# Convolution sums in PSUM, window biases built beside their GEMM, and a late norm in token halves, in a chain of transformer blocks on one Trainium2 core

## The chip, the cores and the metric

The program runs on 1 core of one Trainium2 chip (trn2). The metric is the device time in microseconds (us) of one execution, lower is better; the figure of a kernel is the median of its runs.

## What is computed

The reference runs two blocks on one sequence of 512 tokens of 1024 features, all in f32. The first has two layers: a bidirectional gated delta net (GDN) and a dilated window attention, each followed by a squared-ReLU MLP. The second has two layers with a context of 256 tokens: a Fourier and Hyena mixer and a latent attention (MLA), each followed by a gated feed forward part with a short convolution. Cut to what the change touches:

```python
# first block, layer 0: the input projection of the GDN (24 tiles of q, k, v and 8 of the gate z)
qkv = silu(short_conv(h @ w_in[:, :QKV], conv_w))      # 5 taps, per feature
# first block, layer 1: windows of 128, 512, 2048 tokens, dilated by 1, 4, 16
scores = q @ k.T * scale + rel_bias[bucket(distance)]  # 6 heads per window
# second block, last layer: only the 512 tokens of x are left
h = rms_norm(x, norm2) * (1 + scale) + shift
gate, val = split(h @ w_up)                            # 2 x 2816 features
x = x + g2 * ((silu(dwconv3(gate) + b) * val) @ w_down)
```

## The kernel before, in words

**Layout and stages.** Activations stay in SBUF with features on the 128 partitions and tokens along a row. The program is a list of stages. Each stage (`Core.stage`, L149) is one block with a program for each engine, which talk by semaphores, and it ends with a barrier of all engines; nothing of the next stage starts before it.

**GEMMs.** A weight matrix is cut into chunks of 128x1024 f32 (512 KB). SP loads them in order into a ring of 4 slots (`stream_weights`, `_load`, L188); it runs up to 4 chunks ahead of the stage, into the next GEMM too. For precision each chunk is split into a high and a low fp32r part: ACT copies the high part (`split_high`, L201) and POOL subtracts it for the low part (`split_low`, L207), each into 2 slots, so the high part of chunk n waits until the chunk n-2 has been multiplied. PE multiplies three products per 128x128 block: low weights by high activations (L258), high by low (L259), high by high (L260) (`product`). One output tile of 128 features is one chunk: 8 blocks, so 24 matmuls of 512 columns, each with its own weight load. `multiply_tiles` (L262 to L288) runs the tiles over a ring of 4 PSUM banks (0 to 3); a tile waits until VectorE (DVE) has drained the tile 4 before it (`drained`). With two streams of activations, the matmuls of stream 1 follow those of stream 0 in each tile, and stream 1 has 2 banks (4 and 5).

**Norms.** `Norm` (L306 on) makes the RMS norm first: squares, a sum over the partitions by a matmul with ones (L336), a root on ACT (L340), a reciprocal on DVE, the scaled values (L396), then the shift and the high part on ACT (L365, L366) and the low part on DVE (L390). `LateNorm` (L406 on) multiplies by the gain alone: high part on ACT (L428), low part on DVE (L457); the squares and the root run beside the first two tiles, and 1/rms is applied when a tile is drained (`drain`, L469 and L472), together with two more columns of the GEMM that carry the shift.

**The stage gdn_in** (`gdn_in_stage`, L629 on): DVE copies a tile with its 1/rms into a padded row in SBUF (L665), then sums the 5 taps: a tensor_scalar (L671) and four scalar_tensor_tensor (L673), each in the tile `conv_sum` in SBUF and each waiting for the one before it (class `Order`). ACT takes the Silu of the sum (L703). DVE may start tile n when the Silu of tile n-2 is done. ACT's program is in order: the high part of chunk n+4, then the wait for the sums of tile n and its Silu. After the 24 convolved tiles DVE writes the normed activations for a later stage (`normed`, L480), then drains the 8 gate tiles (L685).

**The stage window_bias** (`window_bias_stage`, L1616 to L1673) stands alone ahead of the GEMM of the windows. SP loads four small tables; PE spreads the bias table by distance (3 matmuls, L1653); DVE adds the window mask (L1674); SP stores the rows to DRAM and reads them back so that each partition is shifted by one element (L1640 to L1645, DRAM to SBUF); PE turns the order of the partitions with a flip matrix (10 matmuls of 384 columns, L1660) and ACT copies them out (L1666). The stage window_in (`copy_gemm_stage`, L1678 on) then multiplies 27 tiles with a `LateNorm`.

**The feed forward part of the last layer** (`ffn_stages`, L2371 on): 22 pairs of tiles, a gate and a value. In layer 0 there are two streams (512 tokens of x, 256 of the context) and a `LateNorm`; in layer 1 (stages ffn1_up and ffn1_down) one stream of 512 tokens, a `Norm` and 2 banks. Two streams of this kind multiply 512 columns and 258 columns (256 tokens and the 2 columns of the shift).

Of the kernel before, what the change touches and what calls it, by code (L numbers as in the profile page):

```python
# [13 lines left out]
P = 128  # L14
T = 512
# [94 lines left out]
class Core:  # L110
# [151 lines left out]
    def multiply_tiles(self, pe, g, streams, drained, norm):  # L262
# [366 lines left out]
def gdn_in_stage(core, g, norm, parts, conv, gate_z, loads):  # L629
# [3 lines left out]
    with ExitStack() as ctx:  # L633
        padded = core.sb("conv_padded", [P, 2, T + 2 * PAD], ctx)
        acc = core.sb("conv_sum", [P, 2, T], ctx)
        taps = core.params("conv").rearrange("p (n j) -> p n j", j=CONV)
        TAPS_ORDER = CONV * g.per
        with core.stage("gdn_in", "loaded", "drained", "convolved", "silued", "dve_order", *Norm.SIGNALS) as (
# [14 lines left out]
            def _(dve):  # L653
# [28 lines left out]
                for n in range(QKV_TILES, g.tiles):  # L682
                    core.tile_sums(dve, g, n)
                    dve.wait_ge(silued, n + 1)
                    dve.tensor_tensor(acc[:, n % 2, :], core.ps[n % RING][:, :], core.rstd[:, 0, :], ALU.mult).then_inc(convolved, 1)  # L685
# [8 lines left out]
            def _(act):  # L694
# [4 lines left out]
                def tile(n, at, turn, out):  # L699
# [3 lines left out]
                    act.activation(out, acc[:, at % 2, :], ACT.Silu).then_inc(silued, 1)  # L703
# [912 lines left out]
def window_bias_stage(core, a, bias0, bias12):  # L1616
# [3 lines left out]
    scratch = core.nc.dram_tensor("bias_by_distance", [HG, 8 * P], F32, kind="Internal").ap()  # L1620
    WIDTHS = (4 * P, 2 * P, 2 * P)
    with ExitStack() as ctx:
        rel = core.sb("rel_table", [BUCKETS, 3 * HG], ctx)
        hot = core.sb("rel_onehot", [BUCKETS, 8 * P], ctx)
        mask = core.sb("window_mask", [HG, 8 * P], ctx)
        rows = core.sb("bias_rows", [HG, 8 * P], ctx)
        flip = core.sb("flip", [P, P], ctx)
        rising0, rising12 = core.sb("rising0", [P, HG, 3 * P], ctx), core.sb("rising12", [P, 2, HG, P], ctx)

        flat12 = lambda t, n: t[:, n // 2, (n % 2) * (HG // 2):(n % 2 + 1) * (HG // 2), :].rearrange("p h j -> p (h j)")  # L1630
        FLIPS = [(rising0[:, h, :], bias0[:, h, :], 3 * P) for h in range(HG)]
        FLIPS += [(flat12(rising12, n), flat12(bias12, n), HG // 2 * P) for n in range(4)]
        with core.stage("window_bias", "loaded", "spread", "masked", "stored", "laid", "flipped", "kept") as (
# [15 lines left out]
            def _(pe):  # L1649
# [7 lines left out]
                for n, (src, _dst, w) in enumerate(FLIPS):  # L1657
                    if n >= 4:
                        pe.wait_ge(kept, n - 3)
# [1691 lines left out]
```

## Time and profile before

| | |
|---|---|
| runs | 3608.68, 3605.53, 3614.42 us, median 3608.68 |
| the profiled execution | 3603.65 us, of which the span is 3601.9 us |
| busy over the span | PE 3231.5 us (90%), PE weight loads 2466.0 (68%), DVE 1620.1 (45%), ACT 1020.0 (28%), POOL 1096.4 (30%) |
| granted TensorE clock | mean 0.943 of full speed |
| DMA | 282.14 MB, 78 GB/s |

A profile row of a group names line, engine and operation, what it writes and reads, how often, its busy time and the mean of one. An idle time is put down to what ended it. A row of the timeline has the start from the beginning of the span, the duration of the merged instructions, engine, line, operation, and how many there are.

### The profile page before, as it was taken

The numbers are of one execution on the slowest core, as the hardware profiler recorded it, in microseconds if no ns is written. First come the engines' busy times: TensorE is split into PE (matmuls) and PEld (weight loads), VectorE is DVE, ScalarE is ACT, GpSimd is POOL, SyncE is SP. The second block draws the span as 40 slices with busy tenths as digits, with TensorE's granted clock in tenths as the row PEclk, the third lists the DMA queues.
The fourth block names the chain that finished last, engine by engine and source line by source line (L and its number), as shares of the span: only waits on it lengthen the run. The fifth ranks groups of instructions, "written<-read, shape, count | busy, mean of one in ns | idle before, by whom it ended". The sixth has DMA issues, their size and how long they took to land. (4 is left out here: it accounts for less than half of the span.)

```text
span 3601.9 us, 53210 instructions
## 1 busy us (share of the span) xinstructions
PE 3231.5 (90%) x20636; PEld 2466.0 (68%) x20636; DVE 1620.1 (45%) x2230; ACT 1020.0 (28%) x1524; POOL 1096.4 (30%) x518
## 2 busy tenths in 40 slices
PE   7887877999979979999798889999999679979999
PEld 5664766787858757878377458888888333358877
DVE  7853543421121534211576247556555355544531
ACT  3322322222222612222120013222223224433322
POOL 3322211444424124444022012222232005534443
PEclk9987998999989979999799999999999879989999
DMA  3215434222222012222212101111111011012222
GB/s 124 76 47 177 143 114 159 88 99 87 99 78 99 30 47 88 99 88 94 91 47 77 59 26 57 64 63 61 57 62 56 33 46 44 23 64 94 98 88 87
DMA packets 78393, 282.14 MB, mean 78 GB/s; under 512 B 9305, under 2 KB 12191, under 8 KB 77228
## 3 DMA queue, kind: packets, MB, share of 16 engines
q1 hardware_dynamic: 77676, 279.52, 23.3%
q8 instruction: 103, 1.69, 0.2%
q10 hardware_dynamic: 576, 0.62, 0.1%
q14 instruction: 38, 0.31, 0.0%
HBM read 270.12 MB, written 2.12 MB: 76 GB/s over the span
## 5 line engine op out<-in xcount | busy, mean ns | idle before, releaser
L207 POOL TENSOR_TENSOR weights_low<-weight_ring,weights_high 128x1024 fp32r<-128x1024 f32 x359 | 897.4, 2500 | 1891.0 <-ACT weights_high L201 1891.0
L201 ACT ACTIVATE weights_high<-weight_ring 128x1024 fp32r<-128x1024 f32 x372 | 391.6, 1053 | 742.9 <-PE bank L260 726.7
L258 PE MATMUL bank<-ffn_in_high,weights_low 128*128 128x512 f32 (+1 forms) x1056 | 376.7, 357 | 14.0 <-DVE ffn_in_low L390 9.0
L259 PE MATMUL bank<-ffn_in_low,weights_high 128*128 128x512 f32 (+1 forms) x1056 | 376.1, 356 | 0.0
L260 PE MATMUL bank<-ffn_in_high,weights_high 128*128 128x512 f32 (+1 forms) x1056 | 376.1, 356 | 0.0
L258 PEld LDWEIGHTS bank<-ffn_in_high,weights_low 128*128 128x128 f32 x1056 | 200.1, 189 | 47.1 <-issue 12.4
L259 PEld LDWEIGHTS bank<-ffn_in_low,weights_high 128*128 128x128 f32 x1056 | 200.1, 189 | 28.2
L260 PEld LDWEIGHTS bank<-ffn_in_high,weights_high 128*128 128x128 f32 x1056 | 199.2, 189 | 28.1
L258 PE MATMUL bank<-mlp_down_high,weights_low 128*128 128x512 f32 x512 | 201.3, 393 | 8.4 <-DVE mlp_down_low L557 8.4
L258 PE MATMUL bank<-mlp_in_high,weights_low 128*128 128x512 f32 x512 | 200.9, 392 | 7.3 <-DVE mlp_in_low L457 6.2
L259 PE MATMUL bank<-mlp_down_low,weights_high 128*128 128x512 f32 x512 | 200.7, 392 | 0.0
L260 PE MATMUL bank<-mlp_down_high,weights_high 128*128 128x512 f32 x512 | 200.6, 392 | 0.0
L259 PE MATMUL bank<-mlp_in_low,weights_high 128*128 128x512 f32 x512 | 200.0, 391 | 0.0
L260 PE MATMUL bank<-mlp_in_high,weights_high 128*128 128x512 f32 x512 | 199.9, 390 | 0.0
L258 PE MATMUL bank<-ffn_down_high,weights_low 128*128 128x512 f32 (+1 forms) x528 | 189.6, 359 | 11.4 <-DVE ffn_down_low L557 11.4
L259 PE MATMUL bank<-ffn_down_low,weights_high 128*128 128x512 f32 (+1 forms) x528 | 189.5, 359 | 0.0
L260 PE MATMUL bank<-ffn_down_high,weights_high 128*128 128x512 f32 (+1 forms) x528 | 188.2, 357 | 0.0
L557 DVE TENSOR_TENSOR ffn_down_low<-ffn_hidden,ffn_down_high 128x1024 fp32r<-128x1024 f32 (+1 forms) x66 | 101.6, 1569 | 190.4 <-ACT ffn_down_high L514 190.4
L557 DVE TENSOR_TENSOR mlp_down_low<-mlp_hidden,mlp_down_high 128x512 fp32r<-128x512 f32 x64 | 44.1, 692 | 295.0 <-ACT mlp_down_high L514 295.0
L258 PE MATMUL bank<-gdn_in_high,weights_low 128*128 128x512 f32 x256 | 106.8, 417 | 43.9 <-DVE gdn_in_low L457 19.8
L619 DVE SCALAR_TENSOR_TENSOR mlp_relu<-bank,rstd 128x512 f32<-128x512 f32 x64 | 44.2, 691 | 214.0 <-PE bank L260 213.5
L673 DVE SCALAR_TENSOR_TENSOR conv_sum<-conv_padded,params,conv_sum 128x512 f32<-128x512 f32 x96 | 118.7, 1237 | 13.9 <-DVE conv_sum L671 0.2
(546 smaller groups left out, 6426.8 us busy)
## 6 DMA issues: line engine op xcount, KB each, us to landing
weight_ring<-in_mod SPq DMA_DIRECT2D x96, 512.0 KB, 4.6
weight_ring<-in_ffn_up SPq DMA_DIRECT2D x88, 512.0 KB, 3.3
weight_ring<-in_mlp_up SPq DMA_DIRECT2D x64, 512.0 KB, 3.3
weight_ring<-in_mlp_down SPq DMA_DIRECT2D x64, 512.0 KB, 3.3
weight_ring<-in_ffn_down SPq DMA_DIRECT2D x44, 512.0 KB, 3.3
weight_ring<-in_gdn_in SPq DMA_DIRECT2D x32, 512.0 KB, 3.3
weight_ring<-in_dswa_in SPq DMA_DIRECT2D x27, 512.0 KB, 3.3
weight_ring<-in_fh_in SPq DMA_DIRECT2D x16, 512.0 KB, 3.3
```

The costliest lines, as they stand in the source:

```text
L201: act.activation(self.high[:, (g.s0 + at) % SPLIT, 0:g.floats], raw, ACT.Copy).then_inc(self.high_ready, 1)
L207: pool.tensor_tensor(self.low[:, slot, 0:g.floats], self.ring[:, (g.c0 + at) % RING, 0:g.floats], self.high[:, slot, 0:g.floats], ALU.subt ...
L258: pe.matmul(bank, wl, ah, start=start, stop=False)
L259: pe.matmul(bank, wh, al, start=False, stop=False)
L260: return pe.matmul(bank, wh, ah, start=False, stop=stop)
L557: last = dve.tensor_tensor(low[:, at % 2, :, lo:lo + tokens], src((n - p * PER_PASS) * KC, KC), high[:, at % 2, :, lo:lo + tokens], ALU.su ...
L619: dve.scalar_tensor_tensor(out=relu[:, at % 2, :], in0=core.ps[at % RING][:, :], scalar=0.0, in1=core.rstd[:, 0, :], op0=ALU.max, op1=ALU. ...
L673: ins = dve.scalar_tensor_tensor(out=acc[:, b, :], in0=padded[:, b, t:t + T], scalar=tap, in1=acc[:, b, :], op0=ALU.mult, op1=ALU.add)
```

## The change

Three edits. (1) In gdn_in the tile `conv_sum` in SBUF is gone; the sums of the taps, and the gate tiles, are written to PSUM banks 4 and 5. (2) The stage window_bias is gone; its steps are a class `DistanceBias` that runs inside window_in: SP loads the tables ahead of the weights, stores the rows after chunk 16 has been asked for and reads them back four chunks later; PE does the 3 matmuls of the table after tile 3 and the 10 flips behind the last tile, with 3 banks in turn in place of 4; DVE adds the mask after draining tile 3; ACT copies the flips out after its last weight split. (3) ffn1_up takes the path that layer 0 had: a `LateNorm` over two streams, here the first and the second 256 tokens of x, with 4 and 2 banks, the drains through `drain`, and the shift added on DVE.

```diff
@@ multiply_tiles
             if n == 1 and norm.late:
                 norm.tensor(pe)
+        if beside:
+            beside.tensor(pe)
         rounds(pe, RING, g.count, RING, tile)
@@ gdn_in_stage
-        acc = core.sb("conv_sum", [P, 2, T], ctx)
+        acc = core.ps[4:6]
...
-                                order(dve.tensor_scalar(acc[:, b, :], padded[:, b, 0:T], tap, None, ALU.mult))
+                                order(dve.tensor_scalar(acc[b][:, :], padded[:, b, 0:T], tap, None, ALU.mult))
...
-                                ins = dve.scalar_tensor_tensor(out=acc[:, b, :], in0=padded[:, b, t:t + T], scalar=tap,
-                                                               in1=acc[:, b, :], op0=ALU.mult, op1=ALU.add)
+                                ins = dve.scalar_tensor_tensor(out=acc[b][:, :], in0=padded[:, b, t:t + T], scalar=tap,
+                                                               in1=acc[b][:, :], op0=ALU.mult, op1=ALU.add)
...
-                    act.activation(out, acc[:, at % 2, :], ACT.Silu).then_inc(silued, 1)
+                    act.activation(out, acc[at % 2][:, :], ACT.Silu).then_inc(silued, 1)
@@ window_bias_stage becomes class DistanceBias
+        self.to = [core.ps[b][:, 0:3 * P] for b in (4, 5, 7)]
+        self.banks = [core.ps[4][0:HG, 0:4 * P], core.ps[5][0:HG, 0:2 * P], core.ps[5][0:HG, 2 * P:4 * P]]
...
+    def turn(self, pe):
+        pe.wait_ge(self.laid, 48)
+        for n, (src, _) in enumerate(self.flips):
+            if n >= len(self.to):
+                pe.wait_ge(self.kept, n - len(self.to) + 1)
+            pe.matmul(self.to[n % len(self.to)], self.flip[:, :], src, start=True, stop=True).then_inc(self.flipped, 1)
@@ copy_gemm_stage
         def _(sp):
+            beside.load(sp)
+            core.stream_weights(sp, g.c0 + g.count // 2)
+            beside.store(sp)
+            core.stream_weights(sp, g.c0 + g.count // 2 + RING)
+            beside.lay(sp)
             core.stream_weights(sp, g.c0 + g.count)
...
             core.split_high_all(act, g, norm)
+            beside.keep(act)
...
-            core.multiply_tiles(pe, g, [(parts, core.ps[0:RING])], drained, norm)
+            core.multiply_tiles(pe, g, [(parts, core.ps[0:RING])], drained, norm, beside)
+            beside.turn(pe)
...
-            rounds(dve, 0, g.tiles, g.per, tile)
+            rounds(dve, 0, RING, g.per, tile)
+            beside.vector(dve)
+            rounds(dve, RING, g.tiles, g.per, tile)
@@ ffn_stages
-    streams = [0, 1] if with_ctx else [0]
-    xs, tokens = (core.x, core.xc if with_ctx else None), (T, TC)
+    streams = [0, 1]
+    first, of_mod = (T, streams) if with_ctx else (T // 2, [0, 0])
+    xs = (core.x[:, :, 0:first], core.xc[:, :, :] if with_ctx else core.x[:, :, first:T])
+    tokens, to = (first, TC if with_ctx else T - first), (0, first)
...
-                            o(dve.tensor_scalar(gates[0], bank(0, j, 0)[:, :], 1.0, None, ALU.mult))
-                            dve.sem_inc(gate_drained, 1)
...
-                            dve.wait_ge(silued, m + 1)
-                            dve.tensor_tensor(dsts[0], gate[0], bank(0, j, 1)[:, :], ALU.mult).then_inc(gated, 1)
-                            dve.wait_ge(gated, m + 1)
-                            dve.sem_inc(value_drained, 1)
```

## Rows read from the trace of the kernel before

**Rows 1.** Busy time in windows, gdn_in: length, PE, PEld, DVE, ACT, POOL, clock, DMA

```profile
38.00:204.00 166.00, 146.50 (x594) 111.75 (x593) 145.18 (x146) 53.41 (x59) 61.58 (x25) 0.98 0.24 78
```

**Rows 2.** Waits of that stretch (40 to 205 us): total us, times, longest

```profile
ACT conv L703 <- DVE conv_sum L673: 87.4, 18, 5.3
```

**Rows 3.** Timeline of DVE in gdn_in

```profile
38.45 0.69 DVE L665 TENSOR_TENSOR conv_padded<-bank,rstd 128x512 f32<-128x512 f32 x1 [0.23 <-DVE rstd L464]
...
87.69 0.49 DVE L671 TENSOR_SCALAR conv_sum<-conv_padded,params 128x512 f32<-128x512 f32 x1 [0.28 <-ACT conv L703]
88.32 5.32 DVE L673 SCALAR_TENSOR_TENSOR conv_sum<-conv_padded,params,conv_sum 128x512 f32<-128x512 f32 x4
94.53 0.49 DVE L671 TENSOR_SCALAR conv_sum<-conv_padded,params 128x512 f32<-128x512 f32 x1 [0.28 <-ACT conv L703]
...
203.88 7.50 DVE L480 SCALAR_TENSOR_TENSOR gdn_h<-x,params,rstd 128x512 f32<-128x512 f32 x8
```

**Rows 4.** Lines L673 and L665: durations in ns, min/median/max, first and last start

```profile
L673 DVE SCALAR_TENSOR_TENSOR conv_sum<-conv_padded,params,conv_sum x96: 750/752/2803, 40.1 to 203.2; 128x512 f32<-128x512 f32 x96
...
L665 DVE TENSOR_TENSOR conv_padded<-bank,rstd x24: 679/684/691, 38.4 to 197.1; 128x512 f32<-128x512 f32 x24
```

**Rows 5.** Timeline of PE in gdn_in, the last gate tiles

```profile
212.19 0.77 PE L258 MATMUL bank<-gdn_in_high,weights_low 128*128 128x512 f32 x1 [4.64 <-DVEq L687]
...
220.03 0.39 PE L258 MATMUL bank<-gdn_in_high,weights_low 128*128 128x512 f32 x1
...
227.03 0.39 PE L258 MATMUL bank<-gdn_in_high,weights_low 128*128 128x512 f32 x1
...
235.89 0.40 PE L260 MATMUL bank<-gdn_in_high,weights_high 128*128 128x512 f32 x1
```

**Rows 6.** Groups of DVE, busy us, mean ns, and one of PE weight loads

```profile
L575 DVE SCALAR_TENSOR_TENSOR x<-bank,mod,x 128x512 f32<-128x512 f32 x32 | 22.9, 747 | 24.5 <-PE bank L260 24.5
...
L2446 DVE TENSOR_SCALAR ffn_padded<-bank 128x512 f32<-128x512 f32 x22 | 15.3, 693 | 84.9 <-PE bank L260 84.9
...
L258 PEld LDWEIGHTS bank<-ffn_in_high,weights_low 128*128 128x128 f32 x1056 | 200.1, 189 | 47.1 <-issue 12.4
```

**Rows 7.** Timeline of window_bias and of the ends of window_in: SP, PE, ACT, DVE

```profile
1017.49 0.34 SPq L1638 DMA_DIRECT2D rel_table<-in_rel_table  x1
...
1020.77 3.45 PE L1653 MATMUL bank<-rel_onehot,rel_table 32*6 32x512 f32 x6 [4.70 <-DMA flip<-in_flip]
...
1037.75 8.52 PE L1660 MATMUL bank<-rising,flip 128*128 128x384 f32 x20 [13.53 <-DMA rising<-bias_by_distance]
...
1042.44 0.49 ACT L1666 ACTIVATE bias<-bank 128x384 f32<-128x384 f32 x1 [0.15 <-PE bank L1660]
...
1046.31 0.49 ACT L1666 ACTIVATE bias<-bank 128x384 f32<-128x384 f32 x1 [0.15 <-PE bank L1660]
1047.52 5.01 ACT L428 ACTIVATE window_in_high<-x,params 128x512 fp32r<-128x512 f32 x8 [0.72 <-PEq L157]
...
1202.04 0.69 DVE L1706 TENSOR_TENSOR window_qkv<-bank,rstd 128x512 f32<-128x512 f32 x1 [4.80 <-PE bank L260]
```

**Rows 8.** Timeline of ffn1_up: ACT at its start, PE in tile 0 and at the end

```profile
3204.78 1.06 ACT L201 ACTIVATE weights_high<-weight_ring 128x1024 fp32r<-128x1024 f32 x1 [5.84 <-PEq L157]
...
3232.53 0.50 PE L258 MATMUL bank<-ffn_in_high,weights_low 128*128 128x512 f32 x1 [0.31 <-DVE ffn_in_low L390]
...
3467.03 0.39 PE L260 MATMUL bank<-ffn_in_high,weights_high 128*128 128x512 f32 x1
```

**Rows 9.** Timeline of ffn0_up: ACT at its start, PE at 258 and 512 columns

```profile
2198.08 5.01 ACT L428 ACTIVATE ffn_in_high<-x,mod_gain 128x512 fp32r<-128x512 f32 x8 [9.19 <-PEq L157]
...
2227.59 0.39 PE L258 MATMUL bank<-ffn_in_high,weights_low 128*128 128x258 f32 x1 [1.46 <-DVEq L2441]
...
2236.09 0.28 PE L258 MATMUL bank<-ffn_in_high,weights_low 128*128 128x258 f32 x1
...
2238.99 0.39 PE L258 MATMUL bank<-ffn_in_high,weights_low 128*128 128x512 f32 x1
```

More of the change, by code:

```diff
@@ L1678, in copy_gemm_stage, with __init__ @@
-def copy_gemm_stage(core, name, g, norm, parts, dst):
-    with core.stage(name, "drained", "copied", *Norm.SIGNALS) as (block, drained, copied, *sems):
-        norm.signals(sems)
+    def __init__(self, core, a, bias0, bias12, ctx):
+        self.core, self.bias0, self.bias12 = core, bias0, bias12
+        self.scratch = core.nc.dram_tensor("bias_by_distance", [HG, 8 * P], F32, kind="Internal").ap()
+        self.rel, self.hot = core.sb("rel_table", [BUCKETS, 3 * HG], ctx), core.sb("rel_onehot", [BUCKETS, 8 * P], ctx)
+        self.mask, self.rows = core.sb("window_mask", [HG, 8 * P], ctx), core.sb("bias_rows", [HG, 8 * P], ctx)
+        self.flip = core.sb("flip", [P, P], ctx)
+        self.rising0, self.rising12 = core.sb("rising0", [P, HG, 3 * P], ctx), core.sb("rising12", [P, 2, HG, P], ctx)
+        self.loads = [(self.rel, a["rel_table"]), (self.hot, a["rel_onehot"]), (self.mask, a["window_mask"]), (self.flip, a["flip"])]
+        part12 = lambda t, n: t[:, n // 2, (n % 2) * (HG // 2):(n % 2 + 1) * (HG // 2), :].rearrange("p h j -> p (h j)")
+        self.flips = [(self.rising0[:, h, :], bias0[:, h, :]) for h in range(HG)] + [(part12(self.rising12, n), part12(bias12, n)) for n in range(4)]
+        self.to = [core.ps[b][:, 0:3 * P] for b in (4, 5, 7)]
+        self.banks = [core.ps[4][0:HG, 0:4 * P], core.ps[5][0:HG, 0:2 * P], core.ps[5][0:HG, 2 * P:4 * P]]
+        self.cuts = [slice(sum(self.WIDTHS[:g]), sum(self.WIDTHS[:g + 1])) for g in range(3)]
@@ new lines, in signals, with load, store, lay @@
+    def signals(self, sems):
+        self.loaded, self.spread, self.masked, self.stored, self.laid, self.flipped, self.kept = sems
+    def load(self, sp):
+        load_beside(sp, self.loads, self.loaded)
+    def store(self, sp):
+        sp.wait_ge(self.masked, 3)
+        sp.dma_start(self.scratch, self.rows[:, :]).then_inc(self.stored, 16)
+    def lay(self, sp):
+        sp.wait_ge(self.stored, 16)
+        sp.dma_start(self.rising0[:, :, :], bass.AP(self.scratch.tensor, 1, [[1, P], [8 * P, HG], [1, 3 * P]])).then_inc(self.laid, 16)
+        for g in range(2):
+            sp.dma_start(self.rising12[:, g, :, :], bass.AP(self.scratch.tensor, (4 + 2 * g) * P + 1, [[1, P], [8 * P, HG], [1, P]])).then_inc(self.laid, 16)
@@ new lines, in tensor @@
+    def tensor(self, pe):
+        pe.wait_ge(self.loaded, 64)
+        for g, cut in enumerate(self.cuts):
+            last = pe.matmul(self.banks[g], self.rel[:, g * HG:(g + 1) * HG], self.hot[:, cut], start=True, stop=True)
+        last.then_inc(self.spread, 1)
+    def turn(self, pe):
[4 more added lines that the diff above has]
+            pe.matmul(self.to[n % len(self.to)], self.flip[:, :], src, start=True, stop=True).then_inc(self.flipped, 1)
@@ new lines, in keep, with vector, copy_gemm_stage @@
+    def keep(self, act):
+        for n, (_, dst) in enumerate(self.flips):
+            act.wait_ge(self.flipped, n + 1)
+            act.activation(dst, self.to[n % len(self.to)], ACT.Copy).then_inc(self.kept, 1)
+    def vector(self, dve):
+        dve.wait_ge(self.loaded, 64)
+        dve.wait_ge(self.spread, 1)
+        for g, cut in enumerate(self.cuts):
+            dve.tensor_tensor(self.rows[:, cut], self.banks[g], self.mask[:, cut], ALU.add).then_inc(self.masked, 1)
+def copy_gemm_stage(core, name, g, norm, parts, dst, beside):
+    with core.stage(name, "drained", "copied", *beside.SIGNALS, *Norm.SIGNALS) as (block, drained, copied, *sems):
+        beside.signals(sems[:len(beside.SIGNALS)])
+        norm.signals(sems[len(beside.SIGNALS):])
@@ L2377, in ffn_stages @@
     wide = JOINT if with_ctx else T
-    late = with_ctx
-    banks = [core.ps[0:RING], core.ps[RING:RING + 2]] if late else [core.ps[0:2]]
-    col0 = (0, CTX0)
+    banks = [core.ps[0:RING], core.ps[RING:RING + 2]]
+    col0 = (0, CTX0 if with_ctx else first)
     with ExitStack() as ctx:
```

104 lines of the change are left out of this document (23 added, 81 removed).

## The prediction

> **What bounds the kernel now.** PE is busy for 90% of the span, so what matters is the time in which it doesn't run its matmuls, and whose fault that is. I read the busy time by window first, then the waits, then the timelines of the three stages that are edited.
>
> In gdn_in the windows view has 594 matmuls in 166 us [rows 1]. A free run of PE there starts 30 matmuls in 7.00 us, 0.2333 us each (220.03 to 227.03 [rows 5]), so 594 are worth 138.6 us and 27.4 us are lost, while DVE is busy for 145 of 166 us. The waits say how: ACT, whose program is in order, sat 87.4 us for the sums of the taps [rows 2], and it splits no further weights meanwhile. DVE's timeline gives its cycle: one tile each 6.84 us (87.69 to 94.53), over all 24 (203.88 - 38.45) / 24 = 6.89 [rows 3], against 24 x 0.2333 = 5.60 us of PE for a tile. DVE is the bound. Of its cycle the tensor_scalar takes 0.63 until the next operation, the four sums are busy 5.32, and the rest with L665 is 0.89. A sum takes 0.750 at the least and its median, but up to 2.80 [rows 4]: four of 0.75 with three gaps of 0.145 would be 3.44, so a tile loses 1.88 us to something that strikes one sum. POOL is splitting weights then. L665, which reads one operand from PSUM, never took over 0.691 in 24 tiles [rows 4]: with one operand in SBUF that something does not strike. The Trainium skill says the same on the page "SBUF — State Buffer", section "Who interferes with whom": a VectorE instruction with at most one SBUF input, outside the two-port modes, does not contend with GpSimd, and one with two does; the trace agrees with it.
>
> In window_bias nothing is done for the GEMMs: it lasts from 1017.49 to the start of window_in at 1047.52, 30.0 us [rows 7]. In ffn1_up the stage starts at 3204.78 and tile 0 gets its last activations only at 3232.53 [rows 8], because the whole norm comes first; from there PE runs without a gap to 3467.03.
>
> **Part 1, sums in PSUM.** Removed is the 1.88 us of the strike, if the one SBUF operand that is left (the padded row) behaves as L665. The trace has no DVE write into PSUM. The nearest row for a sum is L575, the same operation with a pointer scalar and one PSUM input: 0.747 [rows 6], as good as the 0.750 with all in SBUF. From below a sum could take the 0.69 of L665. From above I bound it by twice 0.75, as if the read and the write of one bank took turns. The tensor_scalar loses its fast form (0.49 from SBUF to SBUF): L2446, which reads PSUM, takes 0.693, and I add 0.05 for the pointer scalar (the difference of 0.747 to 0.693): 0.75 with a gap of 0.14. I take 0.75 for all five, the nearest row. New cycle: 0.89 + (4 x 0.75 + 3 x 0.145 = 3.44) + 0.89 = 5.22 us; bounds 4.92 and 8.97.
>
> That is below PE's 5.60, so two ends compete. PE's: it loses the 27.4 us of rows 1, the wait of 4.64 at tile 28, and the 1.5 us by which the last four tiles exceed 4 x 5.60 (212.19 to 235.89 with 0.23, part of it at the low clock that follows the wait [rows 5]); its last matmul would start at 235.89 - 33.5 = 202.4. DVE's: 38.45 + 24 C, then 7.50 for L480 and 0.8 until tile 28 may start, then 22.2 for four tiles: 68.95 + 24 C (for C = 6.89 this gives 234.3, plus the 1.5: the record has 235.89). It passes 202.4 only from C = 5.56. So PE is next in line, and the part saves **33.5 us**. ACT is no bar: a weight split (1.05), at times with a table load (1.3), and POOL's 2.4 us are under 5.60. The load of L480 is already in the formula.
>
> A rule speaks against this part. The Trainium skill, page "Perfetto Trace Analysis", section "Optimizing Scalar/DVE Operations", puts the overhead of a DVE operation at about 60 ns on SBUF and about 125 on PSUM. The rows of reads from PSUM show none of it. An estimate by that page: 65 ns on each of five operations make C 5.55, and the sum stays; on the read and the write of each sum and on the one write (9 times) C is 5.81 and 6 us of the saving are gone.
>
> **Part 2, the biases beside window_in.** Removed: 30.0 us. Added on PE: the 3 table matmuls, 3.45 us in rows 7 at the clock they met there; at the full clock between half of that and all, I take 2.1 in the middle of warm work. Then the 10 flips behind tile 26: at full clock ACT's copies follow each other at (1046.31 - 1042.44) / 6 = 0.645 us with 0.49 busy [rows 7], a pace that PE sets, and three banks still give ACT 1.3 us for 0.49 plus the hand-over. Tile 26's drain ended the stage at 1202.73; the matmuls end at about 1201.84, so 6.45 + 0.15 + 0.49 lead to 1208.9, an addition of 6.3. Ends: 5.5 and 9 us (all ten at the pace of the 8.52 us of rows 7). DVE adds the mask in some 1.6 us between draining tile 3 and tile 4, where it has 5.5 us and needs 0.7: nothing waits. The four table loads pass the weights on SP's queue, where the next weight load waits for a split anyway. The store and the three read-backs stand between weight loads; the store, the reads and their waits took 13.5 us of PE's time before the flips [rows 7]. A load is asked for some 18 us (four tiles less a split) before ACT wants it and needs 3.3; with the read-back ahead of it it is still in time, by a margin of about 1 to 4 us. I count zero. They have ten tiles until the flips. Behind SP's wait for the mask stand only weight loads, and the mask is done some nine tiles earlier. Sum: -30.0 + 2.1 + 6.3 = **-21.6 us**.
>
> **Part 3, the halves.** Start: in ffn0_up, which has this form with 512 and 258 columns, stream 1 of tile 2 gets its bank 29.5 us after ACT's first instruction (2198.08 to 2227.59 [rows 9]). The chain to it is ACT's high parts, squares, DVE's sums, tile 1, root, reciprocal, drain. With 256 columns in place of 512 in stream 0 and a tile of 5.8 in place of 8.3 I make it 6.8 us shorter, 22.7: at 3227.5. Half a tile later tile 3 can start, 3230.4, and tile 4 at about 3236.5. Before, tile 1 started at 3233.33 and tile 4 three tiles of 5.44 later ((3467.26 - 3233.33) / 43 [rows 8]), at 3249.65. Gain 13.1 us.
> Cost: 24 matmuls of 258 columns take 2.90 us (2236.09 to 2238.99 [rows 9]), so a tile of two halves takes 5.80 in place of 5.44: over 40 tiles 14.4 us. The weight load of 189 ns [rows 6] is longer than this pitch of 121 ns, but the run of 24 shows that it overlaps. DVE works some 10 us in a pair of 11.6 with its waits for POOL; its tail behind the last tile is 0.8 us longer. Sum 14.4 + 0.8 - 13.1 = **+2.1 us**, between -2 and +7.
>
> **Sum.** -33.5 - 21.6 + 2.1 = -53.0 us. The profiled execution took 3603.65 us with a span of 3601.9, 5 us under the median of the runs, 3608.68; from the execution the sum leads to 3550.6, and I forecast against the median: **3555.7 us**.
>
> **Rivals.** (a) *DVE stays the bound of gdn_in.* An operation on PSUM costs some 0.1 to 0.15 us more and C is 5.8 to 6.0. The last start is then 208.2 to 213.0, the part saves 28 to 23, and the time is 3561 to 3566. For it: no row shows a write to PSUM. Against: the reads are free. The rule of the Trainium skill quoted above ("Perfetto Trace Analysis"), counted on every access, is this case. (b) *The strike stays*, since the padded row and the pointer scalar are still in SBUF: C = 5.22 + 1.88 = 7.1, last start 239.4, 3.5 us later than before; the time is 3592.7. L665's maximum speaks against it. (c) *The read-back holds up a weight load* or the flips start late, some 5 to 11 us: 3561 to 3567. (d) *Slower.* In gdn_in the sum reads and writes the same bank, and if these take turns C is 8.97: last start 68.95 + 215.3 = 284.2, 48.3 us late, and the time is 3608.7 + 48.3 - 21.6 + 2.1 = 3637.5. It decides from C = 8.2, where it has eaten what the other parts bring and 0.3% more. No row shows such a form, and none hints at it. (e) *The third part does not do what it is for*: it is in the forecast as a small loss already; on its own it would be within the noise.
>
> **Numbers.** Forecast 0.66; (a) 0.18; (c) 0.07; (b) 0.04; (d) 0.02; 0.03 for a start of a stage at the low clock and other losses of some us. 0.3% is 10.8 us, about what a measurement of this kernel can tell from no change: the chances are 0.96 faster, 0.02 within, 0.02 slower. The range takes in (a), (c), the bounds of parts 2 and 3, 5 us by which the median of three runs moves, and not (b) and (d): 3544 to 3575.
>
> **What would show it.** In the changed profile L673 should be 0.75 with a maximum near it, L671 near 0.75, L665 to L665 near 5.6 us on average, ACT's wait for the sums below 20 us, the last matmul of gdn_in near 202. No gap between mlp0's last drain and window_in but the barrier; the last copy of L1666 some 7 us behind window_in's last matmul. In ffn1_up the first matmul two to three us into the stage, tiles at 5.80, the end of the stage later by 1 to 3 us against its start. Wrong it is if L673's maximum stays over 2 us (b), if its median is over 0.85 (a, d), or if PE waits on weights in window_in (c).

## The result, and the profile after

The changed kernel takes 3551.59 us (median; 3550.53 to 3557.45), the kernel before on the same chip 3611.55 us: ratio 0.9845, 95% interval 0.9832 to 0.9858. (The ratio is not the quotient of the two medians, which is 0.9834; the interval holds both.) The profiled execution has a span of 3548.8 us against 3601.9, 53.1 us less, at a granted clock of 0.947 against 0.943. The prediction had a sum of -53.0 us. I read where the 53.1 us come from at the borders of the stages, since a stage ends with a barrier and what lies behind it is only shifted.

| border | before | after | shift |
|---|---|---|---|
| first matmul behind gdn_in | 238.46 | 204.85 | -33.6 |
| ACT's first instruction behind mlp0 (window_bias, now window_in) | 1017.49 | 983.59 | -33.9 |
| first matmul behind window_in | 1203.63 | 1147.87 | -55.8 |
| ACT's first instruction of ffn1_up | 3204.78 | 3153.15 | -51.6 |
| first matmul of ffn1_down | 3471.78 | 3418.92 | -52.9 |

The differences between the lines are the parts: -33.6, -21.9 (from -33.9 to -55.8) and -1.2 (from -51.6 to -52.9). Between 1203 and 3204 us nothing was edited, and 4.1 us were lost there; another 0.3 us were gained between the first two lines; the last section says more on that.

**gdn_in.** Busy time in the window of [rows 1], the waits of [rows 2], and the lines of [rows 4] (durations in ns, min/median/max, first and last start in us; the line numbers in this stage are two higher than before):

```profile
38.00:204.00 166.00, 164.70 (x706) 132.35 (x704) 119.26 (x161) 62.19 (x72) 68.66 (x29) 1.00 0.27 92
```

```profile
ACT weights_high L201 <- PE bank L260: 63.0, 21, 4.1
ACT L201 <- PE bank L260: 21.9, 6, 4.1
...
ACT conv L705 <- DVE bank L675: 9.6, 6, 2.4
```

```profile
L675 DVE SCALAR_TENSOR_TENSOR bank<-conv_padded,params,bank x96: 754/755/758, 40.9 to 165.7; 128x512 f32<-128x512 f32 x96
...
L673 DVE TENSOR_SCALAR bank<-conv_padded,params x24: 753/754/756, 40.0 to 162.1; 128x512 f32<-128x512 f32 x24
...
L667 DVE TENSOR_TENSOR conv_padded<-bank,rstd x24: 682/684/692, 39.0 to 161.1; 128x512 f32<-128x512 f32 x24
```

PE has 706 matmuls in the 166 us in place of 594. A sum's maximum is 758 ns in place of 2803 [rows 4], over 96 of them. ACT waited 87.4 us for the sums [rows 2] and now waits 9.6 (the trace has a second row of this wait, without a tile's name: 23.3 us before, 2.0 now); what it waits for now is PE (63.0 and 21.9 us), which must finish a chunk before its slot is split anew. From the start of this window to the last matmul of the stage no PE matmul has an idle time before it. The bound has moved from DVE to PE. DVE's timeline, against [rows 3]:

```profile
81.89 0.76 DVE L673 TENSOR_SCALAR bank<-conv_padded,params 128x512 f32<-128x512 f32 x1 [0.28 <-ACT conv L705]
82.79 3.46 DVE L675 SCALAR_TENSOR_TENSOR bank<-conv_padded,params,bank 128x512 f32<-128x512 f32 x4
...
87.11 0.76 DVE L673 TENSOR_SCALAR bank<-conv_padded,params 128x512 f32<-128x512 f32 x1 [0.28 <-DVE conv_padded L667]
...
92.34 0.75 DVE L673 TENSOR_SCALAR bank<-conv_padded,params 128x512 f32<-128x512 f32 x1 [0.28 <-ACT conv L705]
...
166.33 8.08 DVE L482 SCALAR_TENSOR_TENSOR gdn_h<-x,params,rstd 128x512 f32<-128x512 f32 x8
```

The cycle is 5.23 us (82 to 87 to 92), and the last convolved tile is done at 166.33, before at 203.88.

**window_in.** Timelines of ACT, PE, DVE and SP's queue, against [rows 7]:

```profile
983.59 5.01 ACT L430 ACTIVATE window_in_high<-x,params 128x512 fp32r<-128x512 f32 x8 [5.78 <-PEq L157]
...
1011.66 1.88 PE L1658 MATMUL bank<-rel_onehot,rel_table 32*6 32x512 f32 x6
1013.47 0.50 PE L258 MATMUL bank<-window_in_high,weights_low 128*128 128x512 f32 x1
...
1013.65 1.34 DVE L1677 TENSOR_TENSOR bias_rows<-bank,window_mask 6x512 f32<-6x512 f32 x3 [1.20 <-PE bank L1658]
...
1056.28 0.33 SPq L1647 DMA_DIRECT2D bias_by_distance<-bias_rows  x1
1061.31 16.89 SPq L188 DMA_DIRECT2D weight_ring<-in_dswa_in  x4
1078.24 0.43 SPq L1651 DMA_DIRECT2D rising<-bias_by_distance  x1
1078.71 1.95 SPq L1653 DMA_DIRECT2D rising<-bias_by_distance  x2
1083.28 5.84 SPq L188 DMA_DIRECT2D weight_ring<-in_dswa_in  x2
...
1139.93 6.61 PE L1666 MATMUL bank<-rising,flip 128*128 128x384 f32 x20
...
1146.58 0.49 ACT L1671 ACTIVATE bias<-bank 128x384 f32<-128x384 f32 x1 [0.15 <-PE bank L1666]
1147.87 0.70 PE L1784 MATMUL bank<-window_qkv 64*128 64x256 f32 x4 [1.33 <-PEq L157]
```

From ACT's start to the next stage's first matmul it is 164.3 us (983.59 to 1147.87), before 156.1 (1047.52 to 1203.63): 8.2 us came in for 30.0 that went out. The weight loads before and behind the read-backs follow each other at the pace of a tile (1077.86 and 1083.28; the first number is the last of the four loads in the row of 1061.31), so the read-backs delayed none, and from 1060 to 1141 us the trace names no wait of PE or of its weight loads.

**ffn1_up.** Timelines of ACT and PE, against [rows 8]:

```profile
3153.15 3.30 ACT L430 ACTIVATE ffn_in_high<-x,mod_gain 128x256 fp32r<-128x256 f32 x8 [5.88 <-PEq L157]
...
3175.02 0.39 PE L258 MATMUL bank<-ffn_in_high,weights_low 128*128 128x258 f32 x1 [1.48 <-DVEq L2450]
...
3413.77 0.28 PE L260 MATMUL bank<-ffn_in_high,weights_high 128*128 128x258 f32 x1
3418.92 0.77 PE L258 MATMUL bank<-ffn_down_high,weights_low 128*128 128x512 f32 x1 [4.87 <-DVE ffn_down_low L559]
```

PE starts at 3154.32, 1.2 us into the stage; it used to start after 18.3 us (3223.08), and tile 0 used to get its last activations after 27.8 us (3204.78 to 3232.53). Stream 1 of tile 2 gets its bank 21.9 us into the stage; from there PE runs without a gap to its last matmul. The stage with its hand-over takes 265.8 us (3153.15 to 3418.92) in place of 267.0.

### The profile page after: what moved, and what is told of

Read it like the earlier page. It is cut to its first block and busy times, and to the rows that moved or that the text cites. A ratio compares the mean times of both kernels' runs of the same rounds, so it can differ in the third digit from the quotient of the medians.

```text
span 3548.8 us, 55536 instructions
## 1 busy us (share of the span) xinstructions
PE 3235.8 (91%) x21694; PEld 2523.9 (71%) x21694; DVE 1634.5 (46%) x2411; ACT 1019.3 (29%) x1530; POOL 1089.9 (31%) x518
## 5 line engine op out<-in xcount | busy, mean ns | idle before, releaser
L258 PE MATMUL bank<-ffn_in_high,weights_low 128*128 128x258 f32 (+2 forms) x1408 | 438.5, 311 | 10.1 <-DVE ffn_in_low L459 6.3
L260 PE MATMUL bank<-ffn_in_high,weights_high 128*128 128x258 f32 (+2 forms) x1408 | 437.8, 311 | 0.0
L259 PE MATMUL bank<-ffn_in_low,weights_high 128*128 128x258 f32 (+2 forms) x1408 | 437.5, 311 | 0.0
L258 PEld LDWEIGHTS bank<-ffn_in_high,weights_low 128*128 128x128 f32 x1408 | 266.8, 189 | 26.2 <-issue 6.8
L259 PEld LDWEIGHTS bank<-ffn_in_low,weights_high 128*128 128x128 f32 x1408 | 267.4, 190 | 14.7
L260 PEld LDWEIGHTS bank<-ffn_in_high,weights_high 128*128 128x128 f32 x1408 | 266.2, 189 | 14.2
L2452 DVE TENSOR_SCALAR ffn_padded<-ffn_padded,ffn_shift 128x512 f32<-128x512 f32 (+1 forms) x88 | 117.5, 1377 | 6.8 <-DVE ffn_padded L474 6.6
```

What stands on the lines that cost most here:

```text
L258: pe.matmul(bank, wl, ah, start=start, stop=False)
L259: pe.matmul(bank, wh, al, start=False, stop=False)
L260: return pe.matmul(bank, wh, ah, start=False, stop=stop)
L2452: o.add(dve.tensor_scalar(dst, dst, shift[:, j % 2, 0, s:s + 1], None, ALU.add))
```

## The experiments

### One part at a time

`e1_conv_only`, `e2_bias_only` and `e3_halves_only` are the kernel before with one of the three parts of the change as the diff above has it, and nothing else.

> The kernel before with the first part alone (sums of the taps in PSUM). My theory: the parts add up, and this one is worth what the trace of the changed kernel shows from the start of gdn_in to that of the next stage, 33.6 us (238.46 - 204.85): about 33.5 us faster, ratio 0.9907, profiled span about 3568.3. Rival: the three parts help one another (a different phase of the weight loads, another clock), and alone it brings 25 us or less, ratio above 0.993.

Measured: ratio 0.9902, interval 0.9887 to 0.9917; last matmul of gdn_in at 201.72, next stage's first at 204.27, 34.2 us earlier than before. The part is worth alone what it is worth in the changed kernel. The span of this one profile is 3573.3 us, 5 us more than I expected, and these 5 us lie behind gdn_in.

> The kernel before with the second part alone (biases inside window_in). My theory: 30.0 us of window_bias go, and window_in grows by the 8.2 us that the changed kernel shows (164.3 us from its start to the next stage's first matmul, before 156.1): 21.8 us faster, ratio 0.9940. Rival: the 8.2 us hold a stall that only falls right in the changed kernel, because part 1 has moved the weight loads; alone it would be 5 us or more off, ratio outside 0.9925 to 0.9955.

Measured: ratio 0.9942, interval 0.9926 to 0.9958, as expected. Its next stage's first matmul is at 1181.14 and window_in's first at 1018.50: 162.64 us, in the changed kernel 162.63 (985.24 to 1147.87). The part costs the same without part 1, whose earlier end shifts all weight loads.

> The kernel before with the third part alone (token halves in ffn1_up). Theory from the trace of the changed kernel: 267.00 us from the stage's start to the first matmul of ffn1_down become 265.8, so 1.2 us faster, ratio 0.9997, no difference that can be measured; in the profile the ramp is some 14 us shorter and 40 tiles cost 5.755 in place of 5.44 us. Rival, as the prediction had it: 2.1 us slower (ratio 1.0006). Second rival: it is one of the larger gains, 5 us or more (ratio below 0.9986), and part 1 or part 2 brings less than I think.

Measured: ratio 0.9999, interval 0.9989 to 1.0008: no difference. In the profile the stage takes 265.78 us (3214.01 to 3479.79), 1.2 us less than before. My expectation of the ratio held, but the ratio can't tell a gain of 1.2 us from a loss of 2.1; the length of the stage in the profile can, and it shows the gain (265.8 us in every profile that has this code).

The three ratios add up to a gain of 0.98 + 0.58 + 0.01 = 1.57%, and the changed kernel has 1.55%. Within what these ratios can tell (0.15% each way), the parts don't touch one another.

### What frees a sum from POOL: its operands or its result

```diff
                             else:
-                                ins = dve.scalar_tensor_tensor(out=acc[b][:, :], in0=padded[:, b, t:t + T], scalar=tap,
-                                                               in1=acc[b][:, :], op0=ALU.mult, op1=ALU.add)
+                                if t % 2:
+                                    ins = dve.scalar_tensor_tensor(out=mid[:, b, :], in0=padded[:, b, t:t + T], scalar=tap,
+                                                                   in1=acc[b][:, :], op0=ALU.mult, op1=ALU.add)
+                                else:
+                                    ins = dve.scalar_tensor_tensor(out=acc[b][:, :], in0=padded[:, b, t:t + T], scalar=tap,
+                                                                   in1=mid[:, b, :], op0=ALU.mult, op1=ALU.add)
```

`mid` is a tile in SBUF, `acc` the two PSUM banks.

> The changed kernel with the sums of the taps alternating between the two memories: tap 0 writes PSUM, sums 1 and 3 read PSUM and write SBUF, sums 2 and 4 read both operands from SBUF and write PSUM. Theory A (two operands read from SBUF make a sum wait for POOL's split): sums 1 and 3 stay at 0.75 us with a maximum near it, sums 2 and 4 show maxima of 2 to 2.8 us. Theory B (it is the write to SBUF that waits): the other way about, sums 1 and 3 show the maxima. Theory C (only a sum that both reads twice from and writes to SBUF is struck): none over 0.8. By A or B half of the sums are open to it, so the cycle of a tile is 5.22 plus up to 1.88 = 7.1 us and the last matmul of gdn_in starts at 203 to 239 us; by C it stays at 202.

The two lines of the sums, the first with one operand from SBUF and its result to SBUF, the second with both operands from SBUF and its result to PSUM:

```profile
L677 DVE SCALAR_TENSOR_TENSOR conv_mid<-conv_padded,params,bank x48: 747/748/751, 40.6 to 190.4; 128x512 f32<-128x512 f32 x48
```

```profile
L680 DVE SCALAR_TENSOR_TENSOR bank<-conv_padded,params,conv_mid x48: 758/1238/2167, 41.5 to 191.2; 128x512 f32<-128x512 f32 x48
```

And the two engines side by side:

```profile
93.72 0.75 DVE L677 SCALAR_TENSOR_TENSOR conv_mid<-conv_padded,params,bank 128x512 f32<-128x512 f32 x1
94.61 1.72 DVE L680 SCALAR_TENSOR_TENSOR bank<-conv_padded,params,conv_mid 128x512 f32<-128x512 f32 x1
```

```profile
93.32 2.45 POOL L207 TENSOR_TENSOR weights_low<-weight_ring,weights_high 128x1024 fp32r<-128x1024 f32 x1 [5.53 <-ACT weights_high L201]
```

POOL's split starts at 93.32. The sum L677 runs at 93.72, wholly inside it, and takes 0.75; L680 starts at 94.61 and ends at 96.33, after the split's end at 95.77. This is no single case: 21 of the 48 sums L677 start inside a split and none takes over 0.751 us; 24 of the 48 sums L680 do, all 24 take 1.7 us or more, and each ends 0.55 to 0.57 us after its split. The kernel before has the same picture. There 24 of the 96 sums start inside a split, one in each tile; these 24 take 2.63 to 2.80 us and end 0.55 us after the split, the others take 0.75. One of them, and its split:

```profile
89.22 2.63 DVE L673 SCALAR_TENSOR_TENSOR conv_sum<-conv_padded,params,conv_sum 128x512 f32<-128x512 f32 x1
```

```profile
88.59 2.71 POOL L207 TENSOR_TENSOR weights_low<-weight_ring,weights_high 128x1024 fp32r<-128x1024 f32 x1 [4.12 <-ACT weights_high L201]
```

In the changed kernel about 40 of the 96 sums start inside a split, and none takes over 0.758. So theory A holds for these sums: what counts is the number of operands read from SBUF, and where the result goes does not decide it. The rule of the Trainium skill that the prediction leaned on (page "SBUF — State Buffer", section "Who interferes with whom") says this of operations outside the two-port modes, and here both of its sides are seen.

That condition matters. A tensor_scalar from SBUF to SBUF is faster for its columns than a sum (0.49 us for 512), and although it reads only one operand, it is struck too. In ffn0_up of the kernel before, 20 of the 22 operations of L2443 over 512 columns start inside a split and take 2.57 to 2.66 us, the other two take 0.49. The first that is struck, and its split:

```profile
2248.83 2.57 DVE L2443 TENSOR_SCALAR ffn_padded<-ffn_padded,ffn_shift 128x512 f32<-128x512 f32 x1 [0.16 <-DVE ffn_padded L472]
```

```profile
2248.72 2.39 POOL L207 TENSOR_TENSOR weights_low<-weight_ring,weights_high 128x1024 fp32r<-128x1024 f32 x1 [5.98 <-ACT weights_high L201]
```

I take this for the page's exception; no trace names an operation's mode. For this form the place of the result does count: the tensor_scalar of the changed gdn_in, which writes to PSUM, starts inside a split 9 times of 24 and never takes over 0.756. It has lost its fast form and with it the exposure.

In e4_alternating_sums half of the sums are open to the strike, and the last matmul of gdn_in starts at 224.87, 22.6 us later than in the changed kernel; its single execution took 3575.99 us. Writing only some of the sums to PSUM would have left most of part 1's gain behind.

### How much room DVE has in gdn_in

```diff
                             if t == 0:
                                 order(dve.tensor_scalar(acc[b][:, :], padded[:, b, 0:T], tap, None, ALU.mult))
+                                order(dve.tensor_scalar(acc[b][:, 0:64], padded[:, b, 0:64], tap, None, ALU.mult))
```

`e6_sixth_op_full` has T (512) in place of 64.

> The changed kernel with tap 0 of every convolved tile written once more for its first 64 columns, an operation of about 0.15 to 0.2 us and a gap of 0.14 in DVE's chain. Theory (PE is the bound of gdn_in and DVE has room up to a cycle of 5.56 us): DVE's cycle goes from 5.23 to 5.5 to 5.6 us, the last matmul of gdn_in stays at 202 to 203 us (202.31 in the changed kernel) and the time doesn't move by more than 1 us. Rival (DVE's chain is still on the path, each added time is seen at the end): 24 times 0.3 us, the last matmul at 209 to 210 us.

> The same with all 512 columns: 0.75 us and a gap of 0.14 more in each tile. Theory: DVE is the bound again with a cycle of 5.23 + 0.89 = 6.12 us; by the prediction's formula the last matmul starts at 68.95 + 24 x 6.12 = 215.9 us, 13.6 us later than in the changed kernel, and ACT's wait for the sums is back at tens of us. Rival (DVE's chain is on the path already): 24 x 0.89 = 21.5 us later, at 223.8. Second rival (PE's four banks take up more than I think): less than 8 us later.

DVE's timeline with the narrow operation, then PE's at the end of gdn_in with the full one:

```profile
83.81 0.76 DVE L673 TENSOR_SCALAR bank<-conv_padded,params 128x512 f32<-128x512 f32 x1 [0.28 <-ACT conv L706]
84.60 0.29 DVE L674 TENSOR_SCALAR bank<-conv_padded,params 128x64 f32<-128x64 f32 x1
...
89.35 0.76 DVE L673 TENSOR_SCALAR bank<-conv_padded,params 128x512 f32<-128x512 f32 x1 [0.28 <-DVE conv_padded L667]
```

```profile
216.05 0.40 PE L260 MATMUL bank<-gdn_in_high,weights_high 128*128 128x512 f32 x1
218.60 0.60 PE L757 MATMUL bank<-w_ab,gdn_h 128*128 128x32 f32 x4 [2.15 <-PEq L157]
```

The narrow operation was dearer than I had said (0.29 us), and the cycle is 5.54 us (83.81 to 89.35), just below the crossover of 5.56. The last matmul starts at 202.39, 0.1 us later than without it, and the span is 3549.5 us: 24 times 0.31 us on DVE (7.4 us) cost nothing that can be seen. ACT waits 49.8 us for the sums here, five times as long as in the changed kernel, and PE loses nothing by it: the length of such a wait does not tell what it costs. With the full one the cycle is 6.02 (its gap is shorter than I had counted) and the last matmul starts at 216.05. The formula 68.95 + 24 C would give 213.4 with this cycle; with my 6.12 it gave 215.9, and that it fits to 0.2 us is in part chance. ACT's wait is at 72.8 us. This single execution is 13.3 us slower (span 3562.1), far from the 21.5 of a DVE that was on the path already. So in the changed kernel DVE's chain has 0.3 us a tile to spare, and less than 0.8.

### The tail of window_in

```diff
             if n >= len(self.to):
                 pe.wait_ge(self.kept, n - len(self.to) + 1)
+            pe.matmul(self.to[n % len(self.to)], self.flip[:, :], src, start=True, stop=True)
             pe.matmul(self.to[n % len(self.to)], self.flip[:, :], src, start=True, stop=True).then_inc(self.flipped, 1)
```

> The changed kernel with each of the 10 flips multiplied twice. Theory: the tail of window_in is PE's own time, two instructions of about 0.33 us for each flip; from the first flip to the next stage's first matmul it grows from 7.9 to 14.5 us, so 6.6 us more in all. Rival (the tail is the hand-over to ACT and the three banks): it grows by 3 us or less, since the second multiply would fill PE's wait.

The tail took 14.39 us (1138.91 to 1153.30) in place of 7.94: 6.45 us more for 10 more flips, 0.645 each, and PE has no idle time between flips in either kernel. PE's own time makes the tail; the three banks and ACT's copies add only what stands behind the last flip. The span grew by 4.0 only (3552.8 us), since other stages ran 2 to 3 us faster in this execution.

### Without the flips

If the tail is PE's time, it goes only with the flips. A row read backwards does what the flip matrix does:

```diff
+        self.copies = [(self.rising0[:, h, :], bias0[:, h, :]) for h in range(HG)]
+        self.copies += [(self.rising12[:, g, h, :], bias12[:, g, h, :]) for g in range(2) for h in range(HG)]
...
-            dve.tensor_tensor(self.rows[:, cut], self.banks[g], self.mask[:, cut], ALU.add).then_inc(self.masked, 1)
+            dve.tensor_tensor(self.rows[:, cut][:, ::-1], self.banks[g], self.mask[:, cut], ALU.add).then_inc(self.masked, 1)
+
+    def keep(self, dve):
+        dve.wait_ge(self.laid, 48)
+        for src, dst in self.copies:
+            dve.tensor_scalar(dst, src[:, ::-1], 1.0, None, ALU.mult)
...
             core.multiply_tiles(pe, g, [(parts, core.ps[0:RING])], drained, norm, beside)
-            beside.turn(pe)
...
-            rounds(dve, RING, g.tiles, g.per, tile)
+            last = g.tiles // g.per * g.per
+            rounds(dve, RING, last, g.per, tile)
+            beside.keep(dve)
+            rounds(dve, last, g.tiles, g.per, tile)
```

The read-backs start one element earlier, and ACT's copies are gone.

> The changed kernel without the flips: DVE writes the masked rows in reversed order, the read-backs start at element 0, and DVE copies them, reading backwards, to their places after tile 23, beside the GEMM (18 copies, some 5 us of DVE, which is idle for 4.9 of each 5.6 us there). Theory: the 10 flips and the last copy are all that stands behind tile 26, so from window_in's start to the next stage's first matmul 164.3 us become about 158.1, 6.2 us less; ratio to the kernel before 0.9828. Rival: the copies have one operand in SBUF but may hold up POOL's split or the drains, and give back 1 to 5 us of it. Second rival: reading backwards costs DVE several times the 0.5 us of a copy, past the four banks' slack of some 16 us, and the kernel is slower than the changed one.

Timelines of DVE and POOL near the end of the stage, and of PE at the next one:

```profile
1127.19 5.54 DVE L1669 TENSOR_SCALAR bias<-rising 128x384 f32<-128x384 f32 x18 [0.30 <-DVE window_qkv L1706]
1132.65 0.68 DVE L1706 TENSOR_TENSOR window_qkv<-bank,rstd 128x512 f32<-128x512 f32 x1
```

```profile
1127.22 2.58 POOL L207 TENSOR_TENSOR weights_low<-weight_ring,weights_high 128x1024 fp32r<-128x1024 f32 x1 [3.00 <-ACT weights_high L201]
```

```profile
1142.14 0.39 PE L260 MATMUL bank<-window_in_high,weights_high 128*128 128x512 f32 x1
1144.19 0.70 PE L1777 MATMUL bank<-window_qkv 64*128 64x256 f32 x4 [1.66 <-PEq L157]
```

The 18 copies take 5.54 us, the drain behind them comes 1.0 us late (PE has four banks and does not notice), and POOL's split under them takes 2.58 in place of 2.41. One row hides in the 5.54: the second copy starts inside this split and takes 2.56 us, where the other five of its size take 0.35.

```profile
1127.47 2.56 DVE L1669 TENSOR_SCALAR bias<-rising 128x384 f32<-128x384 f32 x1
```

It reads one operand from SBUF and writes to SBUF, as L2443 does above, and is struck like it: the first rival was right that the copies and POOL meet. It gives back nothing, because DVE is idle most of the time here. From window_in's first matmul (987.66) to the next stage's first it is 156.53 us in place of 162.63: 6.1 us less, as expected. The ratio is 0.9808, interval 0.9793 to 0.9823, and thus lower than the expected 0.9828. So I ran it again beside the changed kernel.

The last three kernels ran on one chip. `e12_tables_in_gap` is the kernel of `e8_reversed_reads` without the load of the flip matrix, and with this:

```diff
             if n == 1 and norm.late:
+                if beside:
+                    beside.tensor(pe)
                 norm.tensor(pe)
-        if beside:
-            beside.tensor(pe)
```

> The changed kernel once more, beside the two that follow. All theories: ratio to the kernel before 0.9845, within 0.0015.

> The kernel of e8_reversed_reads once more, beside the changed one on the same chip. Theory: it stands 6.1 us (0.17%) below the changed kernel, as the stage window_in alone shows in its trace, so a ratio near 0.9828; the 0.9808 that it had is partly chance. Rival: the reversed copies help elsewhere too, and it stays at 0.9808, some 13 us below the changed kernel.

> The kernel of e8_reversed_reads with the three table matmuls moved from behind tile 3 to behind tile 1, ahead of the norm's matmul with ones, and without the load of the flip matrix. Theory: PE idles 1.76 us there until DVE has added the squares (1000.27 to 1002.03 in that kernel), and the 1.88 us of the table fall into this gap: window_in becomes 1.8 us shorter, from 156.5 to 154.7 us between its first matmul and that of the next stage. Rival: the ramp is set by what DVE and ACT do for the first drains, and PE's time is given back as a wait before tile 4: no gain. In both, the whole moves by less than the runs scatter.

| kernel | median us | ratio to before | 95% interval | window_in, first matmul to the next stage's |
|---|---|---|---|---|
| e10_changed_again | 3550.65 | 0.9826 | 0.9812 to 0.9840 | 162.64 |
| e11_reversed_again | 3545.28 | 0.9814 | 0.9800 to 0.9828 | 156.53 |
| e12_tables_in_gap | 3545.42 | 0.9817 | 0.9803 to 0.9831 | 154.50 |

```profile
998.28 1.88 PE L1656 MATMUL bank<-rel_onehot,rel_table 32*6 32x512 f32 x6
1000.11 1.12 PE L338 MATMUL bank<-window_qkv,ones 128*128 128x512 f32 x2
```

The table now fills the gap ahead of the matmul with ones, which had been 1.76 us long, and the stage is 2.0 us shorter. At 154.50 us it is as long as it was before the biases moved into it (154.46), so their work now costs PE's chain nothing. The expectation for the changed kernel missed by a little (0.9826 in place of 0.9845 with 0.0015 allowed), and that tells how far such a ratio moves from one set of runs to the next; the quotients of the medians are 0.9834 and 0.9833. For the same reason the ratio of e11_reversed_again, 0.9814, can't decide between the 0.9828 of its theory and the 0.9808 of its rival. The difference within the set can: reversed reads are 5.4 us better here by the medians, and the stage itself says 6.1 both times, so the theory holds against its rival of 13 us. The 2.0 us of the last step are in the stage and cannot be seen in the whole. These two kernels are the fastest of this study.

## Why the prediction was right

The forecast was 3555.7 us, the median came out at 3551.59. The mechanisms of parts 1 and 2 were right, with one piece of evidence that did not bear what was put on it; part 3 had the right mechanism and the wrong sign, from small errors in its terms.

**Part 1** (-33.5 forecast, -33.6 found). The step that carried it was the choice of 0.75 us for an operation with one PSUM operand and a PSUM result, of which there was no row. The rows say 0.755 for the sum and 0.754 for the tensor_scalar; the cycle is 5.23 against 5.22, and the last matmul starts at 202.31 against 202.4. Rival (a) is out: with its read and its write in PSUM a sum has a median of 755 ns against the 752 of SBUF [rows 4]. An estimate by the page "Perfetto Trace Analysis" of the Trainium skill (65 ns more for each access) would have had the sum at 0.88, and no row here shows such a price. Rival (b) is out by the maximum of 758 ns, and e4_alternating_sums shows why. The reason that the prediction gave against it was luck: L665's maximum of 0.691 says nothing of the strike, since none of its 24 operations overlapped a split of POOL. Rows that do were there. Of the 8 drains of the gate tiles (L685, the same form) 3 started inside a split and took no more than 0.69, and of the 32 of L575 [rows 6] 6 did and took 0.75. Rival (d) would have needed 1.5 us for the same sum; its cycle of 8.97 also doubles the tensor_scalar, which only writes the bank, and the sums alone would give 8.2. That PE is next in line at a cycle of 5.56 was read off two formulas: at 5.54 nothing is lost, at 6.02 it is 13.7 us. DVE's own formula was off by 2.6 us at the second point, so its constant of 68.95, taken from a kernel whose last tiles waited otherwise, is good to some 3 us only. Two signs failed. The first matmul of ffn1_up was to come two to three us into the stage and comes after 1.2. And L667 to L667 was to be 5.6 us on average, and it is (161.10 - 39.05) / 23 = 5.31. PE starts at 19.88 and has finished some tiles when DVE drains the first one at 39.05, so DVE works off a backlog nearly at its own pace of 5.22; it has not caught up at the 24th tile, whose last matmul starts at 157.51 and whose drain at 161.10. Neither changes a term of part 1's sum.

**Part 2** (-21.6 forecast, -21.9 found). The table matmuls were put at 2.1 us: they hold PE for 1.8 (1011.66 to 1013.47), and from its first to its last weight matmul window_in takes 154.46 us in place of 152.44, so 2.0 more. The flips with the last copy were put at 6.3 (the prediction's own 1208.9 - 1202.7 is 6.2): from the last weight matmul to the next stage's first matmul it is 8.17 us in place of 2.02, so 6.15 more, and without them in e8_reversed_reads it is 2.05. The zero for the store and the read-backs held, and with it rival (c) is out: the read-backs are asked for at 1078.24 and the next weights at 1083.28, and PE has no wait on weights in this stretch. How small the margin is was not tried.

**Part 3** (+2.1 forecast, -1.2 found, the one part where the sign was wrong). The mechanism was right, and its terms were mis-sized. The ramp: stream 1 of tile 2 comes after 21.9 us, not 22.7. The pitch: one tile is 5.76 us (3301.69 to 3307.45 in the same timeline), not 5.80, since a run of 24 half matmuls takes 2.88 and not the 2.90 that one run of ffn0_up had [rows 9]; over 40 tiles this makes 1.6 to 1.8 us. The tail: the last matmul shows -1.6 us (260.6 us after ACT's start in place of 262.2) and the hand-over -1.2, so it costs 0.4 and not 0.8. These are 2.8 to 3.0 of the 3.3 us. A term of 0.04 us multiplied by 40 should be taken from a long stretch, not from one tile. For the whole it doesn't matter: the part alone measures 0.9999.

**Sum.** -53.0 forecast, and -53.1 between the two spans. That these agree to 0.1 us is chance. The three parts come to -33.6 - 21.9 - 1.2 = -56.7 us, 3.7 more than forecast, nearly all of it part 3's; the unedited stages between window_in and ffn1_up took 4.1 us back in this pair of profiles. The ratio of 0.9845 is worth 56 us and the medians differ by 60.0; the -56.7 lies within the interval of 51 to 61 us.

## What to carry to other kernels

When another engine streams through SBUF beside VectorE, count the operands that each VectorE operation reads from SBUF: with two it can be struck (up to 2.8 us for 0.75 here). With one it was not, except for the fast tensor_scalar from SBUF to SBUF, which was (2.6 us for 0.49); with its result in PSUM it was slower (0.75) and safe. A PSUM bank was as good a place for an accumulator as SBUF. Before you take a row as proof that a form is safe, look whether it ever ran beside the other engine. An engine taken off the path pays only up to the next one's pace; work out that crossover first, since it says how much of the gain you can get and how much further work (0.3 us a tile here) the freed engine can then take for nothing. Before work is moved beside a GEMM that bounds, ask which engine it lands on: the 10 flips on PE cost 6.1 us there, the same reordering as reversed reads on the idle VectorE cost none.

## What the runs showed that I had not expected

- Reading a row backwards costs VectorE nothing that these rows show: copies of 384 columns with a reversed source take 0.35 us and those of 128 take 0.21, while the same operation with a forward source takes 0.34 for 256 columns (L2443, the least of them) and 0.49 for 512 [rows 3]. Of the 5.54 us of the 18 copies 2.2 are the one that was struck. The masked rows written backwards (6 partitions) take 1.34 us for 1024 columns, as they do written forwards.
- The stages of small matmuls don't repeat as the GEMM stages do. In e3_halves_only the code ahead of ffn1_up is that of before, and still ACT starts it at 3214.01, not 3204.78. Of these 9.2 us 1.1 arose in the last four tiles of gdn_in (0.3 late by 212.5, 1.4 late at the next stage's first matmul), 4.6 between there and the next GEMM (first matmul 613.81 in place of 607.78), in the GDN's own stages, and most of the rest in MLA. In the GDN's stretch both profiles have 7486 matmuls, at a granted clock of 0.86 before and of 0.84 in e3_halves_only; the clock goes with the length, and what sets it was not tried. Over all thirteen profiles the time from the last matmul of gdn_in to that GEMM's first goes from 368.9 to 376.6 us, with the same code. The end of gdn_in repeats within 1.4 us and the length of window_in within 0.1 over all runs that have the same code there. Where a change is worth less than 0.3%, the length of its stage tells more than the time of the kernel.
- The eight `normed` operations (L482), which read two operands from SBUF, take 8.08 us in the changed kernel and 7.50 before [rows 3]. It is POOL's split again: before, one of the eight starts inside a split (2.87 us in place of 0.74), now two do (1.29 and 2.88), and each ends 0.55 us after its split. Before, they were on the path: PE idled 4.64 us ahead of tile 28 until DVE, behind them, had drained a gate tile at 211.31 [rows 5]. In the changed kernel PE has no idle time there.
